# Transposes and weighted sums of older units ahead of the next unit's logits, in a two-block attention network on one Trainium2 core

## The reference, cut to what matters

```python
logits = jnp.einsum('bnqkgd,bnlkd->bnkgql', qb, kp) * (d ** -0.5) + bias
p = masked_softmax(logits, mask, sink)
out = jnp.einsum('bnkgql,bnlkd->bnqkgd', p, vp)
```

## Time and profile before

| | us |
|---|---|
| device time, median of 3 runs | 2984.72 |
| lowest and highest | 2983.91, 2986.87 |
| the profiled execution, device time | 2982.89 |
| the profiled execution, span from first to last instruction | 2981.1 |
| TensorE matmuls busy | 2936.4 (99%) |
| TensorE weight loads busy | 2403.4 (81%) |
| VectorE busy | 1924.8 (65%) |
| ScalarE busy | 1266.2 (42%) |
| GpSimd busy | 217.6 (7%) |

### The profile page before, as it was taken

The page is one execution under the profiler, slowest core; times in us unless marked ns, Lnnn a source line. Parts: engine busy times, 40 slices in busy tenths (PEclk is TensorE's granted clock), DMA queues, the critical chain, the costliest instruction groups (busy, mean ns, idle before and its releaser), DMA issues.

```text
span 2981.1 us, 37294 instructions
## 1 busy us (share of the span) xinstructions
PE 2936.4 (99%) x14159; PEld 2403.4 (81%) x14159; DVE 1924.8 (65%) x2700; ACT 1266.2 (42%) x2045; POOL 217.6 (7%) x308
## 2 busy tenths in 40 slices
PE   8999999999999999999999999999999999999998
PEld 7897788878888888888887877777888887877877
DVE  5886466668868888888865734454544534666655
ACT  5443354543444444443555223333333324435444
POOL 1000000011001010010100000000000100102000
PEclk9999999999999999999999999999999999999999
DMA  8987956568768878878865733333343624776444
GB/s 271 299 296 270 311 177 189 149 194 279 260 211 267 275 265 275 269 261 275 268 205 172 246 126 113 117 113 121 107 134 121 217 87 141 246 237 202 138 134 160
DMA packets 315426, 611.09 MB, mean 205 GB/s; under 512 B 29373, under 2 KB 90010, under 8 KB 314352
## 3 DMA queue, kind: packets, MB, share of 16 engines
q1 hardware_dynamic: 296012, 544.74, 56.5%
q0 software_dynamic: 18272, 62.64, 6.0%
q10 hardware_dynamic: 964, 1.33, 0.2%
HBM read 567.94 MB, written 41.85 MB: 205 GB/s over the span
## 4 chain that ended last, share of the span: by engine, by line
PE 93%; DVE 3%; ACT 1%; issue 1%; DMA 0%; SPq 0%; POOL 0%; POOLq 0%; ACTq 0%; DVEq 0%
PE acc L686 28%; PE acc L688 27%; PE acc L687 27%; PE acc L1507 3%; PE acc L1477 2%; PE acc L1495 2%; DVE w_lo L508 1%; PE acc L1067 1%; PE acc L1475 1%; PE acc L1455 1%; ACT w_hi L502 1%; PE acc L715 1%; PE acc L781 0%; DMA raw<-in_w_in 0%; PE acc L616 0%
## 5 line engine op out<-in xcount | busy, mean ns | idle before, releaser
L686 PE MATMUL acc<-w_hi,a_hi 128*128 128x512 f32 (+3 forms) x3736 | 1483.0, 397 | 10.3 <-DVE w_lo L508 6.8
L688 PE MATMUL acc<-w_hi,a_lo 128*128 128x512 f32 (+3 forms) x3736 | 1448.2, 388 | 0.0
L687 PE MATMUL acc<-w_lo,a_hi 128*128 128x512 f32 (+3 forms) x3736 | 1446.6, 387 | 0.0
L508 DVE TENSOR_TENSOR w_lo<-raw,w_hi 128x1024 fp32r<-128x1024 f32 (+3 forms) x778 | 932.6, 1212 | 384.4 <-ACT w_hi L502 378.8
L502 ACT ACTIVATE w_hi<-raw 128x1024 fp32r<-128x1024 f32 (+3 forms) x778 | 805.4, 1047 | 731.3 <-PE acc L688 671.3
L686 PEld LDWEIGHTS acc<-w_hi,a_hi 128*128 128x128 f32 x3736 | 703.5, 188 | 167.7 <-issue 21.5
L688 PEld LDWEIGHTS acc<-w_hi,a_lo 128*128 128x128 f32 x3736 | 702.6, 188 | 142.7
L687 PEld LDWEIGHTS acc<-w_lo,a_hi 128*128 128x128 f32 x3736 | 704.2, 188 | 126.6
L545 DVE SCALAR_TENSOR_TENSOR lanes_b<-raw,ct,lanes_b 128x1024 f32<-128x1024 f32 x150 | 189.5, 1304 | 0.0
L545 DVE SCALAR_TENSOR_TENSOR lanes_c<-raw,ct,lanes_c 128x1024 f32<-128x1024 f32 x120 | 156.7, 1348 | 0.0
L1553 ACT ACTIVATE pb<-acc,at_st 128x256 f32<-128x256 f32 (+4 forms) x144 | 71.1, 494 | 139.8 <-DVE at_st L1665 91.8
(11 more groups left out here) (431 smaller groups left out, 1767.8 us busy)
## 6 DMA issues: line engine op xcount, KB each, us to landing
raw<-in_w_mod SPq DMA_DIRECT2D x192, 512.0 KB, 4.8
raw<-in_w_in SPq DMA_DIRECT2D x128, 512.0 KB, 5.0
raw<-in_w_mlp_in SPq DMA_DIRECT2D x128, 512.0 KB, 4.4
raw<-in_w_mlp_out SPq DMA_DIRECT2D x128, 512.0 KB, 5.4
raw<-in_e_w_in SPq DMA_DIRECT2D x104, 512.0 KB, 4.4
raw<-in_w_o SPq DMA_DIRECT2D x64, 512.0 KB, 5.0
raw<-in_o_w_in SPq DMA_DIRECT2D x64, 512.0 KB, 4.8
raw<-in_w_in SPq DMA_DIRECT2D x56, 448.0 KB, 4.6
```

The costliest lines, as they stand in the source:

```text
L508: nc.vector.tensor_tensor(w_lo[:, n % SPLITS, 0:size], raw[:, r % RAWS, 0:size], w_hi[:, n % SPLITS, 0:size].bitcast(F32), ALU.subtract)\
L686: nc.tensor.matmul(o, s.lhs(0, kt, tt), wh, start=kt == 0 and not s.goes_on, stop=False)
L687: nc.tensor.matmul(o, s.lhs(0, kt, tt), wl, start=False, stop=False)
L688: last = nc.tensor.matmul(o, s.lhs(1, kt, tt), wh, start=False, stop=end)
```

## The change

In the method `pe` of `Region` the block that issues the logits of unit u, with its own waits, moves behind the blocks of T (unit u-2) and V (unit u-3). Turns and fill stay behind all three. It applies to every pass of all three regions. No instruction is added or taken away, and ACT, DVE, POOL and SP keep their orders.

```diff
                     for u in range(p.U + 3):
-                        if u < p.U:
-                            w, v = p.units[u], p.u0 + u
-                            if v >= 2:
-                                pe.wait_ge(p_done, v if w.pair else v - 1)
...
-                            last.then_inc(s_done, 1)
                         if 0 <= u - 2 < p.U:
                             w, v = p.units[u - 2], p.u0 + u - 2
                             bank = self.tbanks[v % len(self.tbanks)]
...
                                                         start=x == 0, stop=x == len(w.v) - 1)
                             last.then_inc(o_done, 1)
+                        if u < p.U:
+                            w, v = p.units[u], p.u0 + u
+                            if v >= 2:
+                                pe.wait_ge(p_done, v if w.pair else v - 1)
...
+                            last.then_inc(s_done, 1)
                         for feed, x in p.turns.get(u, ()):
                             feed.need(pe, x)
                             feed.turn(pe, x)
                         self.fill(pe, p, u)
```

More of the change, by code:

```diff
@@ L1510, in pe @@
                             last.then_inc(o_done, 1)
+                        if u < p.U:
+                            w, v = p.units[u], p.u0 + u
+                            if v >= 2:
+                                pe.wait_ge(p_done, v if w.pair else v - 1)
+                            if p.exact is not None and u in p.exact:
+                                pe.wait_ge(jl_done, p.jw0 + p.exact[u])
+                            bank = 4 + v % 2
+                            n = len(w.q)
+                            for x in range(n):
+                                if w.pair:
+                                    last = nc.tensor.matmul(acc[:, 4 + x, 0:w.keys], w.q[x], w.k[x], start=True, stop=True)
+                                else:
+                                    last = nc.tensor.matmul(acc[:, bank, 0:w.keys], w.q[x], w.k[x], start=x == 0,
+                                                            stop=x == n - 1 and w.bias is None)
+                            if w.bias is not None:
+                                b, c0 = w.bias
+                                last = nc.tensor.matmul(acc[:, bank, c0:w.keys], ident[:, :], b,
+                                                        start=False, stop=True)
+                            last.then_inc(s_done, 1)
                         for feed, x in p.turns.get(u, ()):
```

## The result

| | before | after |
|---|---|---|
| device time, median (four runs of each, same chip) | 2984.31 us | 3029.23 us |
| lowest and highest | 2982.55, 2986.87 | 3026.65, 3030.99 |
| ratio, 95% interval | | 1.0152 [1.0139, 1.0165] |
| profiled execution: device time, span, clock | 2982.89, 2981.1, 0.998 | 3030.99, 3029.2, 0.996 |

What follows compares the result with a forecast made beforehand. The prediction took TensorE's set instruction order, busy 99% of the span, to bound the kernel, so each new wait is lost time. Terms 9 + 5 + 16.6 + 3.5 sum to 34 us, giving 3018 us, own range 3006 to 3032, whole range 2999 to 3040.

Steps and rivals of the forecast that it cites:

- The sum of T's and V's waits: Sign over the whole kernel: TensorE's waits in transposes and weighted sums together should come to some 40 us.
- The evacuation in C1 unit 5: Pass C1: evacuation chain of 4.77 us, behind a split and the next pass's rotation, outlasts fill and transpose; stall 2.3 us.
- Two signs: TensorE's busy time should stay unchanged; a clock below 1.00 in passes C and D would show the prediction wrong.
- what ends a run of float32 matmuls: Order within the group in at1 and at2: changes 168 times, taken as 0, bounds -8 to +8 us.
- faster: Rival, all passes: banks handed over earlier, so waits for splits and evacuations shrink; 2976 us, chance 5%.
- at1's seven slots: at1, where a step ends and the fill is one triple: stalls of 0.6 us, two with ACT late by 0.25; 3.5 us.
- hidden after all: Rival: if weight loads measure TensorE's limit, waits of 0.3 to 2 us vanish in its slack; 2985 us, chance 7%.
- Only the waits for copies: Rival: evacuation chains are shorter than taken, leaving mostly the waits for ACT's copies; +18 us, 3001, chance 18%.
- B: 5 + 0.4 + 3.9 forecast: B passes: copy stalls of 512-key units 5 us, of 256-key units 0.4, evacuation chains 3.9; sum 9.
- Pair passes: 5 forecast: A0 to A3: 0.9 us in A0 and A1, 3.5 in A2 and A3, 0.7 on an existing wait; sum 5.
- a rival of its own with 12%: Clock falls behind close waits: ten stretches cost 16 us, or D2 and D3 some 30; 3033 to 3060, chance 12%.
- C and D, 20.3 for 16.6: C and D passes: copy waits 11.2 us plus evacuations 8.0, less 2.6 of stalls already there; sum 16.6.

Runs made afterwards that it cites:

- the runs by region: New order in one region only, the rest as before the change: at1 2988.05 us, pair passes 2992.71, B 2995.92, C and D 3002.68; before 2982.56.
- t_ahead: Only the transposes moved ahead of the logits in all passes (order T, L, V, fill), against the kernel before: 2995.74 us, ratio 1.0040.
- v_ahead: Order V, L, T, fill in all passes, so only the weighted sum is ahead of the logits, against the kernel before: 3031.01 us, ratio 1.0163.
- only_at3: New order in passes C and D alone, old order elsewhere, against the kernel before: 3002.68 us, ratio 1.0066.
- only_a: New order in the four pair passes A0 to A3 alone, old order elsewhere, against the kernel before: 2992.71 us, ratio 1.0033.
- evac_ahead: Changed order on TensorE, plus DVE's evacuation one iteration sooner in at1 and at2: 3036.54 us, ratio 1.0176 to the kernel before.

## Why the prediction was right, and where its sizes were off

**The mechanism.** The waits named in the prediction are there: T waits for the copy by 0.24 to 0.28 us in 15 units of B, by 0.78 and 0.84 in D1; the fill of four triples in B2 has none; V waits for `oA`, `oB`, `oC`; in at1 there are waits at five step ends (0.41, 0.64, 0.65, 0.49, 0.49) and nowhere else. The sum of T's and V's waits was forecast at some 40 and is 35.0. The evacuation in C1 unit 5, forecast at 2.3, is the 1.95 of the list. Two signs came out the other way. TensorE's busy time was to stay unchanged and rose by 21 us, and a clock below 1.00 in passes C and D was named as a sign of being wrong, and it is 0.98 there. The waits are the main cause all the same, as the runs by region and t_ahead show, but not the whole of it: the forecast had the clock at nothing, and the clock has some 4 of the 45 us.

Some numbers of the prediction were wrong without moving its sum: what ends a run of float32 matmuls changes in the 144 iterations that have both L and T, not 168 times, V's waits for evacuations were 7.0 and not 5.4, the terms of the rival "faster" make 2974 and not 2976, and at1's seven slots of 0.6 less twice 0.25 make 3.7 and not 3.5.

The rival "hidden after all" (the Trainium skill, "Perfetto Trace Analysis", section "Identifying the Most-Contended Engine") is refuted in its reading for this kernel: weight loads are busy for 80%, and 26 us of new waits cost 45, more than their own length and not less. "Only the waits for copies" falls too: V's waits for evacuations grew from 7.0 to 17.9. "Faster" falls with the waits for split weights, which went from 6.8 to 7.3 and not down.

**The missing 11 us.** What was off are sizes of the sum's terms, in three places for the most part.

*B: 5 + 0.4 + 3.9 forecast, 12.1 measured.* The stall of a 512-key unit was taken as 0.32 and is 0.40 in the unit above. Its chain is as predicted: the copy ends 2.79 us after the start of the bias matmul (2217.86 to 2220.65), 2.78 before. What covers it is shorter: bias and fill have room for T after 2.53 us (2220.39), where the sum had 0.43 and 2.17, because the fill follows the bias 0.25 after its start instead of 0.43 and loses only 0.1 of that again. Units with 256 keys, for which 0.06 each was forecast, have no wait in the list, but from the fill's start to T 2.42 us where it was 2.26: up to 0.16 of a stop has no row, since PE's idle time is counted from a modelled end that lies 0.16 behind the point at which the next instruction could have started. v_ahead's weight loads above show such a wait directly. This is also part of why the busy time rose by 21 us: up to 0.16 of each stall is booked as busy, which makes at most 6 us for the 38 waits that the lists have more than before. Matmuls at the lower clock (below) last longer too; the rest of the 21 I can't assign.

*Pair passes: 5 forecast, 8.5 measured.* A0 has no wait in the list at all and grew by 0.76. Part of that is the order itself. In the pair passes a group of L, T and V without any wait, from the last fill matmul ahead of it to the second one behind it, takes 2.39 us in the changed kernel where it took 2.34, and 2.63 where it took 2.57. t_ahead has the same 2.39 and 2.63, and there A0, A1 and A3, without new waits in them, grew by 0.5 us each. So the order costs some 2 us over four pair passes. It is dearest where V has L on 64 rows behind it (0.54 us where V to the fill took 0.37) and cheaper between T and V (0.22 for 0.27). The other 1.5 us of the excess are waits, listed or hidden under the 0.16, and I can't split them further. In at1 the differences nearly cancel (V +0.08, L -0.08).

*The clock: 0 forecast, some 4 us measured.* It had a rival of its own with 12%, which expected 16 or 30 us from many places; it came in three. In C0 two waits follow each other:

```profile
2756.71 0.63 PE L1476 MATMUL acc<-ident,pb 128*128 128x128 f32 x4 [1.48 <-ACT pt L1562]
2758.45 1.29 PE L1488 MATMUL acc<-vC,pt 128*128 128x128 f32 x8 [1.12 <-DVE oC L1650]
2759.40 0.77 PE L1504 MATMUL acc<-kCT,qCT 128*128 128x512 f32 x1
2759.97 0.63 PE L1504 MATMUL acc<-kCL,qCT 128*128 128x512 f32 x1
```

A matmul of 512 columns takes 0.63 us here instead of 0.40. The windows behind that place, and behind the 1.95 of C1 and the 1.99 of D1:

```profile
2760.00:2767.00 7.00, 7.00 (x27) 5.67 (x26) 5.69 (x11) 3.90 (x7) 1.19 (x3) 0.81 0.52 157
2895.00:2899.00 4.00, 3.80 (x14) 3.30 (x15) 1.16 (x4) 0.28 (x1) 0.00 (x0) 0.60 0.02 4
...
2818.00:2822.00 4.00, 3.94 (x14) 2.92 (x12) 3.19 (x11) 2.21 (x4) 0.00 (x0) 0.66 0.00 0
```

The granted clock falls to the lower level (1.2 GHz) for part of the stretch behind each. In C0 logits and fill there took 1.43 and 6.33 us for 0.78 and 5.46, which is 1.5 us more; D1 grew by 3.6 us with the fall and by 2.0 in only_at3, where the clock stayed at 1.00 behind nearly the same waits.

What decides whether the clock falls is open. Before and only_a have the same instructions in D1, in the old order, and the same wait of 1.96 us. The first row and window are only_a's, the second window is that of before:

```profile
2862.02 1.13 PE L1511 MATMUL acc<-kvD,pt 128*128 128x128 f32 x8 [1.96 <-DVE oD L1654]
...
2862.00:2867.00 5.00, 4.98 (x23) 4.49 (x24) 0.98 (x3) 0.13 (x1) 0.00 (x0) 0.66 0.01 3
...
2852.00:2857.00 5.00, 4.52 (x28) 4.09 (x29) 2.47 (x7) 0.59 (x1) 0.00 (x0) 1.00 0.02 5
```

The clock fell in one and not in the other, and D1 took 1.6 us longer for it. In only_at3 it stayed at 1.00 behind a wait of 1.98 with two of 0.79 and 0.85 shortly ahead, so its expectation's "behind waits of 2 us and more" doesn't hold as a rule, and neither does a rule by how close the waits stand. Executions of one and the same kernel differ as well: only_at3's four took 2999.9 us at a mean clock of 0.998 to 3005.0 at 0.995. So the 4 us are what the profiled execution shows and no fixed price of the order. The Trainium skill, "TensorE: Matmul & The Clock Gate", section on the clock gate, ties the clock to how busy TensorE was recently. That each of these falls stands behind waits agrees with it; which waits bring one on, no run here shows.

Outside the passes the span grew by another 2.1 us. 1.3 of them lie between at1 and A0, where both kernels have a wait of 3.4 us and the clock behind it is 0.83 over 10 us before and 0.66 in the changed kernel; only_a, with at1 as before, has 0.66 too.

at1 came out at 5.1 for 3.5: its five listed waits are 2.7, with up to 0.16 hidden in each 3.5, and the rest I can't assign. C and D, 20.3 for 16.6, differ by about what the clock took there (some 4 us); only_at3, with two falls and not three, has 20.1 as well, so this is good to 1 or 2 us only.

## What to carry to other kernels

In a software pipeline whose bound engine never stops, ask of every instruction that can wait: what stands on that engine between the event that starts the chain (here L) and the waiting instruction. Moving L behind T and V took blocks out of that stretch; putting back one ahead of T and two ahead of V (t_ahead) got 32 of the 45 us back. The stall is the largest excess over all chains, so covering one of two equal chains better gains nothing (v_ahead), and another engine's late evacuation may be what lets it run ahead (evac_ahead). Look for the iteration where a step's end cuts the fill short: giving it its share was worth more (4 us) than any order tried.

## What the runs showed of the hardware that was not expected

An idle time in the list understates a stop: it starts at the modelled end of a 512-column matmul, 0.39 us after its start, where the next one could have started at 0.23. A stop of up to 0.16 us has no row on PE, and can be seen on the weight loads, which are listed as waiting (0.37 at 2217.89 above), or in the distance between starts. Restarting costs a little more: four V matmuls of pass B, to the L behind them, took 0.55 us behind such a stop in v_ahead and 0.45 without one in the changed kernel. What stands behind a V of four matmuls changes its time: 0.54 us to an L on 64 rows, 0.45 to an L on 128 rows, 0.37 to the fill.

The same instructions with the same wait of 1.96 us in pass D1 left the clock at 1.00 in one kernel and brought it to the lower level in another, at a price of 1.6 us. Times of single passes are to be compared with the granted clock beside them.
